# Streaming encoder trunk on one core: paired prompt scores on 64 array rows, and waits filled at five places by reordering

## The reference, cut to what matters

```python
def fox_attend(q, k, v, cq, ck, qpos, kpos):          # forgetting attention, 16 heads of 64
    s = einsum('bqhd,bkhd->bhqk', q, k) * (64 ** -0.5)
    s = s + cq - ck                                   # running sums of the forget logs
    s = where(kpos <= qpos, s, -inf)
    p = softmax(s)
    return einsum('bhqk,bkhd->bqhd', p, v)

x = layer_norm(ALPHA * x + mixer(x));  x = layer_norm(ALPHA * x + (silu(a) * u) @ w_out)

def hgrn_mix(x, S0, ...):                             # 8 heads of 128 x 128 state
    # q, forget, value and gate projections; per chunk: decayed scores, outputs, new state
    o = o * rsqrt(mean(o^2) + eps) * norm_g * silu(gate);  return o @ w_out, S_final

def pool_mix(x, hist, pos, w_pool, scale):            # windows of 2, 4, 8, 16 frames
    z = window_mean(x) - x;  return (z @ w_pool) * scale, last_15_rows
```

## Time and profile before

| | |
|---|---|
| median of 3 runs | 1956.31 us |
| profiled execution | 1953.8 us, span of its instructions 1952.1 us |
| TensorE busy | 97% of the span, 12232 matmuls |
| VectorE, ScalarE, GpSimd busy | 50%, 37%, 12% |
| mean granted TensorE clock | 0.982 of 2.4 GHz |
| HBM traffic | 131 GB/s over the span |

### The profile page before, as it was taken

The page is one execution under the profiler, slowest core; times in us unless marked ns, Lnnn a source line. Parts: engine busy times, 40 slices in busy tenths (PEclk is TensorE's granted clock), DMA queues, the critical chain, the costliest instruction groups (busy, mean ns, idle before and its releaser), DMA issues.

```text
span 1952.1 us, 29476 instructions
## 1 busy us (share of the span) xinstructions
PE 1895.8 (97%) x12232; PEld 1693.6 (87%) x12232; DVE 984.1 (50%) x1577; ACT 715.0 (37%) x1118; POOL 229.1 (12%) x360
## 2 busy tenths in 40 slices
PE   8999999999999999899999999999999999999996
PEld 8877799998888887699998899998897777999985
DVE  4356463443567778644443754443544565444333
ACT  4236433333254554233332233332232463433321
POOL 4113151000011222130000100000030230000000
PEclk9899999999999999899999999999989999999998
DMA  7246344443353433354433344443354562444331
GB/s 256 96 170 216 113 131 129 130 129 121 112 159 101 131 112 102 86 153 130 126 125 128 111 127 126 124 129 129 119 177 141 171 215 80 140 130 126 125 128 65
DMA packets 179173, 259.43 MB, mean 133 GB/s; under 512 B 14685, under 2 KB 122349, under 8 KB 179040
## 3 DMA queue, kind: packets, MB, share of 16 engines
q1 hardware_dynamic: 160752, 195.61, 31.7%
q0 software_dynamic: 18288, 61.94, 9.9%
HBM read 243.20 MB, written 13.19 MB: 131 GB/s over the span
## 4 chain that ended last, share of the span: by engine, by line
PE 92%; DVE 3%; ACT 2%; issue 1%; DMA 1%; SPq 0%; POOL 0%; ACTq 0%; DVEq 0%; POOLq 0%
PE ps L1488 14%; PE ps L1489 14%; PE ps L1490 14%; PE ps L1500 11%; PE ps L1498 11%; PE ps L1499 11%; PE ps L1682 2%; PE ps L1792 1%; PE ps L1551 1%; PE ps L1554 1%; PE ps L1553 1%; PE ps L1516 1%; PE ps L1779 1%; PE ps L1768 1%; PE ps L1730 1%
## 5 line engine op out<-in xcount | busy, mean ns | idle before, releaser
L684 DVE TENSOR_TENSOR w_lo<-w_raw,w_hi 128x1024 fp32r<-128x1024 f32 x370 | 453.6, 1231 | 746.9 <-ACT w_hi L390 745.8
L390 ACT ACTIVATE w_hi<-w_raw 128x1024 fp32r<-128x1024 f32 x370 | 389.6, 1059 | 857.9 <-DMA w_raw<-in_w_ffn_in_dram 371.6
L1488 PE MATMUL ps<-xT_hi,w_hi 128*128 128x384 f32 x1568 | 528.5, 337 | 2.7 <-DVE w_lo L684 2.2
L1489 PE MATMUL ps<-xT_lo,w_hi 128*128 128x384 f32 x1568 | 527.9, 337 | 0.0
L1490 PE MATMUL ps<-xT_hi,w_lo 128*128 128x384 f32 x1568 | 527.8, 337 | 0.0
L1488 PEld LDWEIGHTS ps<-xT_hi,w_hi 128*128 128x128 f32 x1568 | 295.4, 188 | 3.6 <-DVE w_lo L684 2.3
L1489 PEld LDWEIGHTS ps<-xT_lo,w_hi 128*128 128x128 f32 x1568 | 295.2, 188 | 0.4
L1490 PEld LDWEIGHTS ps<-xT_hi,w_lo 128*128 128x128 f32 x1568 | 295.3, 188 | 0.0
L1500 PE MATMUL ps<-w_hi,hT_lo 128*128 128x512 f32 x528 | 210.6, 399 | 0.0
L1499 PE MATMUL ps<-w_lo,hT_hi 128*128 128x512 f32 x528 | 208.0, 394 | 0.0
L1498 PE MATMUL ps<-w_hi,hT_hi 128*128 128x512 f32 x528 | 207.5, 393 | 0.0
(11 more groups left out here) (302 smaller groups left out, 2198.7 us busy)
## 6 DMA issues: line engine op xcount, KB each, us to landing
w_raw<-in_w_ffn_in_dram SPq DMA_DIRECT2D x352, 256.0 KB, 3.2
w_raw<-in_w_ffn_out_dram SPq DMA_DIRECT2D x176, 256.0 KB, 2.8
w_raw<-in_w_fox_in_dram SPq DMA_DIRECT2D x96, 256.0 KB, 3.1
k_c<-in_cache_fox_k_dram POOLq DMA_DIRECT2D x32, 512.0 KB, 4.8
v_c<-in_cache_fox_v_dram POOLq DMA_DIRECT2D x32, 512.0 KB, 4.0
w_raw<-in_w_hgrn_in_dram SPq DMA_DIRECT2D x64, 256.0 KB, 3.0
w_raw<-in_w_fox_out_dram SPq DMA_DIRECT2D x32, 256.0 KB, 2.8
gb<-in_ln_g_dram POOLq DMA_DIRECT2D x8, 512.0 KB, 4.0
```

Of the source, the lines that this page charges most:

```text
L390: nc.scalar.activation(w_hi[:, slot, :], w_raw[:, slot, :], ACT.Copy).then_inc(hi_ready, 1)
L684: V.tensor_tensor(w_lo[:, slot, :], w_raw[:, slot, :], w_hi[:, slot, :].bitcast(F32), ALU.subtract).then_inc(lo_ready, 1)
L1488: mm(out, w_hi[:, slot, cols], x_hi[:, k, :], start=k == 0, stop=False, skip_group_check=True)
L1489: mm(out, w_hi[:, slot, cols], x_lo[:, k, :], start=False, stop=False, skip_group_check=True)
```

## The change

It has five parts, each at a place of its own; the arithmetic stays the same except that the zero rows of `qz` are no longer multiplied.

1. *Keys.* The first cached keys are copied out at unit 22 before the weight of that slot, and the last two weights (`LATE = 2`) are prepared after the attention loop rather than before it.
2. *Pairs.* `p_scores(k)` runs at even steps for heads 2k and 2k+1: bias and mask of both, then four products on 64 rows each. `p_out(k)` moves to the head of odd step 2k+3, its consumers move with it, and `pT_p` gets four buffers.
3. *Sums.* Head 0's `turn_logs` follows slot 6's unit, and its `sums` stand inside the units of slots 7, 8 and 9.
4. *Pieces.* Behind head 7's steps TensorE runs half of output unit 3 and four pieces of the second half's units 0 and 1 (tiles 0 and 1), which the tail then skips. Head 7's `updates(7,1)` and VectorE's `sample_states` move back, and VectorE prepares two weights in slots 35 and 39 instead of three in 35, 37 and 39.
5. *Buffer.* The pooling norm's gain and bias get a buffer of their own (`gb_p`), loaded ahead of the last four units of the layer before; the average of tile 2 goes between `product(0)` and `product(1)`, and the splits of the first tiles before weights. GpSimd then loads `gb` for the norm after next, and the stores of kept prompt and sample rows count on two semaphores.

```diff
+LO_AT = {35: 0, 39: 1}
+LATE = 2
+        gb_p = sb("gb_p", [P, 2, D], after("hT_hi"))
@@ ScalarE, normed_x @@
                 rstd_of(n, 0)
                 if n in AVERAGED:
+                    transposed_tile(n, 2)
                     last_w_hi(START[n // 2 - 1]["down"], CF)
@@ ScalarE, fox @@
                 for u in range(6 * CU):
-                    if (u + 1) % CU:
+                    if u == 6 * CU - 2:
+                        act.wait_ge(*at(f["ktr"], 1))
+                        act.wait_ge(*at(f["c_lo"], 3))
+                        nc.scalar.activation(ktc[:, 0:2, 0:PAST], ...)
+                    if (u + 1) % CU and u < 6 * CU - LATE:
                         w_hi_of(m0 + u + RING)
...
-                        if n >= 3:
-                            act.wait_ge(*at(f["o"], (n - 1) // 2))
-                        nc.scalar.activation(pT_p[:, (n - 1) % 2, :], ...)
+                        if n >= 5:
+                            act.wait_ge(*at(f["o"], (n - 3) // 2))
+                        nc.scalar.activation(pT_p[:, (n - 1) % 4, :], ...)
...
-                for u in range(2 * CU - TAIL):
+                for u in range(-LATE, 2 * CU - TAIL):
                     w_hi_of(START[i]["out"] + u + RING)
@@ VectorE, normalise_tile @@
+                if n in AVERAGED:
+                    dve.wait_ge(gb_p_loaded, 32)
@@ VectorE, fox @@
+                    if u == 6 * CU - 2:
+                        key_sides(0, 1)
+                    if (u + 1) % CU and u < 6 * CU - LATE:
                         w_lo_of(m0 + u + RING)
...
-                    if n >= 3 and n % 2:
-                        k = (n - 3) // 2
+                    if n >= 4 and n % 2 == 0:
+                        k = n // 2 - 2
...
-                        dve.wait_ge(*at(f["scores"], n + 1))
+                        dve.wait_ge(*at(f["scores"], n // 2 + 1))
@@ VectorE, hgrn @@
-                    if kb == 2:
+                    if kb == 2 and hb < HG - 1:
                         sample_states(hb, 0)
...
-                    if u - 2 in OUT_AT:
-                        w_lo_of(out0 + OUT_AT[u - 2] + RING)
+                    if u in LO_AT:
+                        w_lo_of(out0 + LO_AT[u] + RING)
...
+                sample_states(HG - 1, 0)
                 low_out(HG - 1)
+                sample_states(HG - 1, 1)
@@ VectorE, pool @@
+                split_tile(n + 1, 0)
                 w_lo_of(out0 + 2)
-                split_tile(n + 1, 0)
+                split_half(n + 1, 1, 0)
                 w_lo_of(out0 + 3)
-                split_half(n + 1, 1, 0)
-                dve.wait_ge(*at(f["stored"], 16 * (DB + 1)))
+                dve.wait_ge(*at(f["stored_s"], 16 * DB))
@@ GpSimd, kept_inputs @@
+                pool.wait_ge(unit_used, START[i - 1]["down"] + 2 * CF - TAIL)
+                pool.dma_start(gb_p[:, 0, :], ln_g[i, 0, :].partition_broadcast(P)).then_inc(gb_p_loaded, 16)
+                pool.dma_start(gb_p[:, 1, :], ln_b[i, 0, :].partition_broadcast(P)).then_inc(gb_p_loaded, 16)
@@ TensorE, tail_tm @@
+                            if (t, v) in done:
+                                continue
                             last = tm(m + v, u + v, kk, t, bank0, x_hi, x_lo, nk)
@@ TensorE, fox @@
-                def p_scores(h):
...
+                def p_scores(k):
+                    for e in range(2):
+                        h = 2 * k + e
+                        if k:
+                            pe.wait_ge(*at(f["exp"], h - 1))
+                        out = ps[:, S_BANK[e], 0:T]
+                        mm(out, sel_p[:, h:h + 1].broadcast_to([CROWS, P]), c_p[:, :], start=True, stop=False, ...)
+                        mm(out, ident_r[:, :], causal_r[:, :], start=False, stop=False, ...)
+                    for lo, hi, n in ((0, P, P), (P, T, SEQ)):
+                        for e in range(2):
+                            rows = slice(HD * e, HD * e + HD)
+                            last = mm(ps[:, S_BANK[e], lo:hi], qz[rows, e, k, lo:lo + P], kT[rows, k, 0:n], ...)
+                    last.then_inc(f["scores"][0], 1)
...
                     if n >= 2:
                         s_fold(n - 2)
-                    if n < HEADS:
-                        p_scores(n)
+                    if n >= 3 and n % 2:
+                        p_out((n - 3) // 2)
+                    if n < HEADS and n % 2 == 0:
+                        p_scores(n // 2)
...
-                    if n >= 2 and n % 2 == 0:
-                        p_out(n // 2 - 1)
                     if n < HEADS:
                         s_pairs(n)
+                p_out(KD - 1)
@@ TensorE, hgrn @@
+                def second(u, t):
+                    pe.wait_ge(lo_ready, out0 + CU + u + 1)
+                    for kk in range(2):
+                        tm(out0 + CU + u, u, kk, t, 0, xT_hi, xT_lo, KD)
...
+                    if u == SLOTS - 3:
+                        pe.wait_ge(*at(f["oT_lo"], HG - 1))
+                        pe.wait_ge(lo_ready, out0 + CU)
+                        for t in range(NTOK):
+                            tm(out0 + CU - 1, CU - 1, 0, t, 4, xT_hi, xT_lo, KD)
+                        pe.wait_ge(*at(f["exp"], 6 * HG))
+                        second(0, 0)
+                    if u == SLOTS - 2:
+                        second(0, 1)
+                        second(1, 0)
                 turn_out(HG - 1)
+                second(1, 1)
+                updates(HG - 1, 1)
+                pe.wait_ge(*at(f["oT_lo"], HG))
+                for t in range(NTOK):
+                    last = tm(out0 + CU - 1, CU - 1, 1, t, 4, xT_hi, xT_lo, KD)
+                last.then_inc(unit_used, 1)
                 pe.wait_ge(*at(f["snew"], 2 * HG))
-                out_product(i, len(OUT_AT))
+                out_product(i, CU, ((0, 0), (0, 1), (1, 0), (1, 1)))
@@ TensorE, pool @@
                 product(0)
+                average_tile(n, 2, normed(n - 1))
                 product(1)
-                average_tile(n, 2, normed(n - 1))
```

More of the change, by code:

```diff
@@ L494, in fox @@
                         nc.scalar.activation(kv_tok[:, 1, 0, WCOLS:D], ps[:, 4, :], ACT.Copy).then_inc(f["v_a"][0], 1)
[L495 removed]
+                    if (u + 1) % CU == 0 and u < 6 * CU - LATE:
                         w_hi_of(m0 + u + RING)
                 act.wait_ge(*at(f["kstored"], 16 * 2))
[L499 to L500 removed]
+                for n in range(HEADS + 3):
+                    if 2 <= n <= HEADS + 1:
                         m = n - 2
@@ L886, in fox @@
                         V.tensor_copy(kv_tok[:, 1, 1:NTOK, WCOLS:D], ps[:, 5:7, :]).then_inc(f["v_d"][0], 1)
-                    if (u + 1) % CU == 0:
+                    if (u + 1) % CU == 0 and u < 6 * CU - LATE:
                         w_lo_of(m0 + u + RING)
-                for n in range(HEADS + 2):
+                for n in range(HEADS + 3):
                     if 1 <= n <= HEADS:
@@ L1484, in unit_fm @@
                         wait_x(k)
+                    if amid is not None and kk == 1:
+                        amid()
                     for n in range(4):
@@ L1625, in ffn, with out_product @@
                 tail_tm(2 * i + 1, s["down"] + 2 * CF - TAIL, CF - TAIL, 4, hT_hi, hT_lo, KF)
-            def out_product(i, first=0):
+            def out_product(i, first=0, done=()):
                 for u in range(first, CU):
@@ L1945, in hgrn @@
                         updates(hb, 0)
-                    if kb == 3:
+                    if kb == 3 and hb < HG - 1:
                         updates(hb, 1)
-                    if ka == 0:
+                    amid = (lambda: sums(0, 2 * ka - 2)) if ha == 0 and ka else None
+                    if ka == 0 and ha:
                         turn_logs(ha)
-                    if ka is not None and ka >= 1:
+                    if ka and ha:
                         sums(ha, 2 * ka - 2)
```

90 lines of the change are left out of this document (42 added, 48 removed).

## The result

| | before | after |
|---|---|---|
| median of the runs | 1956.05 us (1955.57 to 1956.8) | 1937.76 us (1934.43 to 1940.62) |
| profiled execution, its span | 1953.8, 1952.1 us | 1939.37, 1937.6 us |
| mean granted clock of the profiled execution | 0.982 | 0.981 |
| TensorE busy | 97% | 1884.6 of 1937.6 us, 97% |

The ratio is 0.991 with a 95% interval of 0.9897 to 0.9922: 18.3 us less by the medians, 15 to 20 by the interval. The forecast was 22.0 us less, 1934.3; the range held the time.

The account below looks back on a forecast made before the run. The prediction took TensorE, busy 97% of the span, as the bound. Its terms for parts 1 to 5, 5.0, 5.8, 1.0, 7.0 and 3.2, sum to 22.0 us off 1956.3: 1934.3 us, range 1926 to 1944.

Parts of the forecast that it names:

- rival 2: Starts of attention give nothing, as the value load or store holds `s_out(0)` as long as before; 1939.3 us, chance 0.08.
- lower bounds: Low ends of the parts' gains, said to give 16 us together, the 64-row case left out.
- odd step (4.53): Attention loop: fold and values, 1.04 us, fit under the 1.3 us chain, so the step stays at 4.53 us.
- the even step's filler: Attention loop: fold, bias and mask twice, paired products and mode cost sum to 1.79 us, making the step 5.01 us.
- the cap on the clock's cost: Start of attention: a 1.2 GHz stretch falling behind `s_out(0)` could cost up to 1.4 us.
- the bound itself: Start of attention: the new values' load landing near 143.5 limits the keys' gain to 3.3 us per layer.
- The new wait: Recurrence, slot 8: 2.4 us of wait for copies of unit 7's banks, with no sums in front.
- that chain of 18 us: Recurrence's end: VectorE's norm chain from output unit 3's end to `first_pair`, none of its steps getting shorter.
- Rival 3: Slower: the clock falls inside the attention loop, some 3.5 us more per slow step, 2032 us at worst; chance 0.04.

Follow-up runs that it names:

- e2: Part 2 (pairs) alone on the kernel before: 1950.47 us, ratio 0.9979.
- e1: Part 1 (keys) alone on the kernel before: 1954.43 us, ratio 0.9994.
- e7: The changed kernel with the values' product back in the even step and two buffers of pT_p: 1946.41 us, ratio 0.9954.
- e8: The changed kernel with the new values loaded first, ahead of the 1 MB store of the values: 1928.05 us, ratio 0.9858.
- e12: Part 1 (keys) alone on the kernel before, with the new values loaded first: 1943.48 us, ratio 0.994.
- e5: Part 3 (sums) alone on the kernel before: 1953.11 us, ratio 0.9992.
- e6: The changed kernel with the products of a pair's two heads on all 128 rows, without row groups: 1938.96 us, ratio 0.991.
- e9: The kernel of e8 with the store of the last head's sample states held until output unit 9's weight is prepared: 1927.76 us, ratio 0.986.
- e3: Part 4 (pieces) alone on the kernel before: 1950.14 us, ratio 0.9972.
- e4: Part 5 (buffer) alone on the kernel before: 1951.04 us, ratio 0.9975.

## Why the prediction was right, and where its terms were off

The forecast was right in direction, size and the places of the waits, on a sum in which three terms were too high (parts 1, 2 and 4) and one too low (part 3). Some of it is luck. By the profiled pair the five terms are worth 4.0 + 0.4 + 2.1 + 4.8 + 3.4 = 14.7 us of the 22.0, and the measured 1937.76 lies nearer to rival 2's 1939.3 than to the forecast's 1934.3. A slip in the text changes nothing of this: its lower bounds, with 5.8 for the pairs, add up to 17.1 us, not 16.

**Part 2, pairs**: 5.8 said, 4.3 measured by the steps of the changed kernel and of e2 (14 x 0.31; the stretches of the table, a little shorter than the loops, have 4.0 and 3.8). Mechanism and odd step (4.53) were right. The step that failed is the sum of the even step's filler, 1.79 us: I took 0.80 for bias and mask twice and 0.65 + 0.2 for products and mode. Measured are 0.80 (156.88 - 155.99 = 0.89, of which 0.09 are the mode's), 0.09 and 0.86, in all 1.89 us with the fold. 0.1 us in each of 14 steps makes the missing 1.4. The Trainium skill's *TensorEngine Tiling (Array Packing)*, Key Properties, has tiles that run in parallel and a drain at a change of mode. The first shows in this case, as 0.86 instead of 1.31 us; the 0.09 us on entering fits the second.

**Part 1, keys**: 5.0 said, 0.4 in the profiled pair (3.7 + 0.7 less the steps' 2.1 + 1.9), about 1 in e1. The place was right: transposes said near 139.5 and seen at 138.85, `s_out(0)` said near 143.5 and seen at 143.16, waits of 1.4 and 2.3 us said and 1.28 and 2.45 seen. With no low clock behind the new wait the part gave 3.1 and 2.6 us (e7), not under the 2.5 taken. What failed was the cap on the clock's cost, "up to 1.4": the low clock behind `s_out(0)` cost 1.5 us in layer 0 and 4.4 in layer 3, 10 us long there. Rival 2, which says the starts give nothing, describes the profiled pair and e1 better than the forecast does, though for another reason than it gave: the load did move (issued at 139.45, where near 139.9 was said), and the clock took the gain back. And the bound itself was no bound of the layer: e8 and e12 show 5.6 us or more a layer, once the load of the new values is out of the way.

**Part 3, sums**: 1.0 said, 2.1 measured in the profiles of the changed kernel and e5. The new wait was said to be 2.4 us and is 2.23; the doubt was whether a low clock follows it. It did in e6 and e9 (1.5 us each, -0.6 and -0.5 over the stage) and not in the changed kernel, e5, e7 and e8. The 1.0 was a mean of two outcomes, of which one came.

**Part 4, pieces**: 7.0 said, 4.8 in the changed kernel, 3.9 in e3's trace, 5.5 by its ratio. The end of the recurrence is as worked out: no wait over 0.7 us in it (the longest is 0.62, at 772.09), and the residual behind unit 3 starts at 790.30 instead of 801.34, 11.0 earlier, of which 4.0 come from earlier stages: 7 us in this one, where 7.8 was said. What failed is the step "that chain of 18 us [...] no step of it gets shorter": one got longer. Moving the last state updates behind output pieces brought their 0.5 MB store next to the load of unit 9's weight, 0.7 us ahead of the unit's end, where before it lay 9.3 us ahead. I had counted the queues for the moved weights, but not the DMA that a moved update sets off. From that residual to `first_pair` it is 20.5 us instead of 18.2. In the tail TensorE idles 4.7 us in one wait, where some 5 in three were said.

**Part 5, buffer**: 3.2 said, 3.4 and (e4) 2.9 measured.

**Not in the sum**: the middle of the recurrence lost 2.4 us and the forget logits of layer 3 gained 1.7. Neither is shown to be the change's: kernels that leave these stages as they were have both. The logits' stretch has one of two lengths in the runs, by where its low clock ends. The collision of VectorE's op with GpSimd's masked values cost 1.3 us or more in nine of the thirteen profiled executions of this study (the changed kernel, e1 to e4, e9 to e12), and nothing in the one of before; so the profiled pair (14.4 us) understates the gain that the medians show (18.3). That the one op holds the other is read from their ends; no run tests it. Why it is VectorE's op in one execution and GpSimd's in another is open.

**Rival 3** fell: the loop ran at full clock (1.00 between 160 and 170 us), with 0.18 us holes in each odd step.

*TensorE: Matmul & The Clock Gate*, Why this matters for your kernels (the Trainium skill), asks for gaps under some 3 us to keep the clock. The trace disagrees: the granted clock fell behind waits of 2.45 and 2.50 us in the changed kernel and of 2.70 in e1, all under that, and stayed at 2.4 GHz behind 2.44 us in e7. Both the changed kernel and e7 have a wait of 1.28 us shortly before.

## What to carry to other kernels

Read the next wait behind the one you remove with the same care, and remove both together: here the keys alone gave about 1 us, the keys with the value load 11 to 12 (the value load alone was not run). Follow every moved instruction to the DMA it sets off, and look at which load it now starts beside. And lay traces side by side by the number of the matmul: by time alone e6 would have said that row groups are worth nothing, and e9 that the store costs nothing.

## What the runs showed of the hardware

- Two fp32 products on 64 rows each ran at once when they lay in different halves of the rows: they start 0.006 us apart, and eight of them take 0.86 us instead of 1.31 for eight on 128 rows, with 0.09 us for entering. The saving is under half because the first pair is followed after 0.21 us and the last after 0.31, where the same sizes on all rows take 0.11 and 0.22 (e6).
- The granted clock fell to 1.2 GHz behind waits of 1.43 us (the changed kernel, at 676) to 2.80 us (before, at 784) in some executions and not in others, with the same instructions around them: behind the 2.23 us of slot 8 in e6 and e9, and not in the changed kernel, e5, e7 and e8. Behind a single wait it stayed down from 3 to 10 us. A forecast can give it a chance and a price, not a place.
- An op of VectorE that takes 0.35 us elsewhere took 2.84 us beside an op of GpSimd of 1.91 us, and ended 0.2 us behind it (e1: 2.86 beside 1.91). In before, e5 and e8, at the same offset, GpSimd's op took 3.3 us and VectorE's 0.35.
- A 0.5 MB store issued 0.7 us before the end of the unit that frees a weight's slot went with that weight's preparation starting 6.5 to 6.8 us behind that end (the changed kernel, e3, e8) instead of 3.8, and the second of its two 256 KB loads landing after 6.0 to 6.3 us instead of 3.2; with the store held back (e9) it was 3.8 and 3.3.
